# A transformer layer on one Trainium2 core: block sums stored in two parts, and the last layer norm and last product reordered

## The reference, cut to what matters

```python
def layer_norm(x, g, b):
    mu = x.mean(-1, keepdims=True)
    var = jnp.square(x - mu).mean(-1, keepdims=True)
    return (x - mu) * lax.rsqrt(var + EPS) * g + b

y_x = concat([mo, go, co]) @ w_o
x = layer_norm(ALPHA * x + mx[:, 2] * y_x, ln1_g, ln1_b)
u = x * (1.0 + mx[:, 4]) + mx[:, 3]
y_x = jnp.square(jax.nn.relu(u @ w1)) @ w2
x = layer_norm(ALPHA * x + mx[:, 5] * y_x, ln2_g, ln2_b)
```

## Time and profile before

| what | us |
|---|---|
| median of 3 runs | 3297.54 |
| lowest and highest run | 3292.43, 3299.11 |
| the profiled execution | 3291.43 |
| its span in the profile | 3289.6 |
| TensorE busy | 3093.5 (94%) |
| VectorE busy | 2354.3 (72%) |
| GpSimd busy | 1470.7 (45%) |
| ScalarE busy | 1365.4 (42%) |

### The profile page before, as it was taken

How to read it: one execution, slowest core, us unless ns; L and a number is a source line. 1 busy time by engine, 2 the same in 40 slices (tenths; PEclk the granted TensorE clock), 3 DMA queues, 4 the chain that set the end, 5 groups by cost and what they waited for, 6 DMA issues and landing times. The chain is left out here.

```text
span 3289.6 us, 38729 instructions
## 1 busy us (share of the span) xinstructions
PE 3093.5 (94%) x13713; PEld 2283.2 (69%) x13713; DVE 2354.3 (72%) x3209; ACT 1365.4 (42%) x1931; POOL 1470.7 (45%) x857
## 2 busy tenths in 40 slices
PE   6999958999999999999998897999999999999996
PEld 3888845565565655656565775888788888887885
DVE  4344447777777777777765888777778768887778
ACT  3222222434344343444442435655555554344432
POOL 1233301576665766765662445333333223444453
PEclk8999977999999999999998998999999999999998
DMA  6222378123332223230214577444734488777873
GB/s 236 62 88 85 90 239 271 53 57 83 87 82 74 56 61 87 67 80 14 54 35 165 224 260 292 161 158 156 291 144 150 152 311 293 289 265 275 299 288 137
DMA packets 235708, 515.51 MB, mean 157 GB/s; under 512 B 26704, under 2 KB 101840, under 8 KB 223312
## 3 DMA queue, kind: packets, MB, share of 16 engines
q1 hardware_dynamic: 224688, 472.39, 43.0%
q10 hardware_dynamic: 10848, 40.90, 3.5%
HBM read 356.64 MB, written 156.57 MB: 156 GB/s over the span
## 5 line engine op out<-in xcount | busy, mean ns | idle before, releaser
L1032 DVE TENSOR_REDUCE h_mpart<-a_mx 128x1 f32<-128x512 f32 x920 | 568.3, 636 | 260.6 <-PE a_mx L1121 251.7
L978 POOL TENSOR_TENSOR a_acc_p<-a_acc_p,a_pf 128x1024 f32<-128x1024 f32 x240 | 582.0, 2425 | 234.2 <-ACT a_pf L1014 213.0
L1014 ACT ACTIVATE a_pf<-a_sc 128x1024 f32<-128x1024 f32 x432 | 443.0, 1026 | 475.5 <-PE a_sc L1147 470.2
L2148 PE MATMUL f_bank<-slot_hi,f_wx 128*128 128x512 f32 x1280 | 401.0, 390 | 9.0 <-DVE f_wx L1931 7.0
L2081 POOL TENSOR_TENSOR f_work<-raw_rows 128x512 f32<-128x512 f32 x160 | 220.9, 1382 | 369.8 <-DVE f_wx L1931 366.4
L2090 POOL TENSOR_TENSOR f_y<-f_y,raw_rows 128x1024 f32<-128x1024 f32 x80 | 222.0, 2776 | 333.2 <-DMA raw_rows<-in_w 333.2
L2148 PE MATMUL f_bank<-slot_lo,f_wx 128*128 128x512 f32 x896 | 350.0, 391 | 0.0
L2148 PEld LDWEIGHTS f_bank<-slot_hi,f_wx 128*128 128x128 f32 x1280 | 240.9, 188 | 60.4 <-DVE f_wx L1931 7.4
L2156 PE MATMUL f_bank<-slot_hi 128*128 128x512 f32 x672 | 263.9, 393 | 12.4 <-DVE slot_lo L1938 12.4
L1952 DVE TENSOR_TENSOR f_work<-f_work,f_bank 128x512 f32<-128x512 f32 x256 | 174.4, 681 | 134.3 <-ACT f_work L1821 123.1
L2156 PE MATMUL f_bank<-slot_lo,slot_hi 128*128 128x512 f32 x672 | 263.6, 392 | 0.0
(11 more groups left out here) (288 smaller groups left out, 6545.1 us busy)
## 6 DMA issues: line engine op xcount, KB each, us to landing
raw_rows<-s_hx SPq DMA_DIRECT2D x112, 512.0 KB, 4.1
f_y<-in_w SPq DMA_DIRECT2D x112, 512.0 KB, 5.2
raw_rows<-in_w SPq DMA_DIRECT2D x80, 512.0 KB, 5.8
raw_rows<-in_w SPq DMA_DIRECT2D x32, 1024.0 KB, 4.8
s_hx<-stream SPq DMA_DIRECT2D x128, 256.0 KB, 2.7
s_hx<-f_work SPq DMA_DIRECT2D x96, 256.0 KB, 2.0
a_wa<-in_w_ada SPq DMA_DIRECT2D x8, 2048.0 KB, 9.0
s_mix<-low SPq DMA_DIRECT2D x96, 128.0 KB, 2.5
```

The lines of the kernel that those rows point to most:

```text
L978: nc.gpsimd.tensor_tensor(acc[:, :], left[:, :], pf[(b * KT + kt) % NPF][:, :], ALU.add).then_inc(added_p, 1)
L1014: nc.scalar.activation(pf[n % NPF][:, :], sc[n % 2][:, :], ACT.Exp, scale=SCALES[0 if is_mla(b) else 1]).then_inc(exped, 1)
L1032: nc.vector.reduce_max(mpart[b % 2][:, s, k:k + 1], mx[c % 2][:, 0:CHUNKS[k][1]], AX.X).then_inc(mx_read, 1)
L2148: mm = nc.tensor.matmul(by_pair(bank[:, m % 8, :]), w[:, k], x[s][:, :, k * P:(k + 1) * P], start=(k == 0 and j == 0), stop=(k == 3 and j ...
```

## The change

In the mixing stage the seven positions of pair p are made in two parts (`HALVES`): positions 0 to 3 behind tile 2p + 2, positions 4 to 6 behind tile 2p + 3, on GpSimd, ScalarE and VectorE, and their stores likewise. On ScalarE, `stream` of an even tile stands behind the root and the second part of the next tile. `load_m` goes from ScalarE's queue to SyncE's, ahead of the store of `x1`.

In the MLP's second half the products come in another order; the layer norm is two instructions on VectorE (subtract mean, times `ln_g`; times the root, plus `ln_b`), so that ScalarE's centring, GpSimd's addition and two small steps of `norms` are gone; of the last product the first three chunks are made for all four token tiles and the other five tile by tile; its quarter gets gate and residual ahead of it (`before_last`), and then only the gated bank is added; stores of the output count on three semaphores, so that the first copies of the second half wait for their own four tiles.

```diff
+        HALVES = (range(0, 4), range(4, NP))
@@ sync
+            load_m(0)
             sp.dma_start(ln_cols[:, :], a["ln1_cols"]).then_inc(cols_in, 16)
+            load_m(1)
...
             for s, t in enumerate(TILE):
+                if s + 2 < TT:
+                    load_m(s + 2)
                 sp.wait_ge(x1_set, s + 1)
                 sp.dma_start(g.x1[t * P:(t + 1) * P, :], x1[s % 2]).then_inc(x1_stored[s % 2], 16)
...
+                if s >= 2:
+                    store_sums(s // 2 - 1, s % 2)
@@ scalar
             for s in range(TT):
-                if s:
-                    stream(s - 1)
-                act.wait_ge(var_set, s + 1)
-                nc.scalar.activation(rstd[:, :], var[:, :], ACT.Sqrt).then_inc(std_set, 1)
+                if s and s % 2 == 0:
+                    stream(s - 1)
+                root(s)
+                if s >= 2:
+                    highs(s // 2 - 1, s % 2)
+                if s % 2:
+                    stream(s - 1)
                 if s + 2 < TT:
                     load_x(s + 2)
-                    load_m(s + 2)
-                if s and (s - 1) % 2:
-                    highs((s - 1) // 2)
@@ vector
                 work(s)
-                if s and (s - 1) % 2:
-                    lows((s - 1) // 2)
+                if s >= 2:
+                    lows(s // 2 - 1, s % 2)
@@ gpsimd
-                if s and (s - 1) % 2:
-                    sums((s - 1) // 2)
+                if s >= 2:
+                    sums(s // 2 - 1, s % 2)
@@ stage_mlp
-        ORDER2 = (5, 3, 2, 4, 1, 6, 7)
+        ORDER2 = (2, 4, 3, 1, 6, 5, 7)
-        DVE_ADDS = {5: (), 3: (("12", 1),), 2: (("22", -1),), 4: (("11", 1), ("21", 1)), 1: (("11", 1), ("22", 1)), 6: (("22", 1),), 7: (("11", 1),)}
-        ACT_FIRST = {5: (("12", 1), ("11", -1)), 3: (("22", 1),), 2: (("21", 1),), 4: (), 1: (), 6: (), 7: ()}
+        DVE_ADDS = {2: (), 4: (("21", 1),), 3: (("22", 1),), 1: (("11", 1), ("22", 1)), 6: (("22", 1),), 5: (("12", 1), ("11", -1)), 7: (("11", 1),)}
+        ACT_FIRST = {2: (("21", 1), ("22", -1)), 4: (("11", 1),), 3: (("12", 1),), 1: (), 6: (), 5: (), 7: ()}
-        PRES = {3: ("12",), 4: ("21",), 6: ("22",), 7: ("11",)}
+        PRES = {4: ("21",), 6: ("22",), 5: ("12",), 7: ("11",)}
@@ vector, scale
-                dve.wait_ge(centred, k + 1)
-                nc.vector.tensor_tensor(yacc[t], yacc[t], ln_g, ALU.mult).then_inc(scaled, 1)
+                nc.vector.scalar_tensor_tensor(out=yacc[t], in0=yacc[t], scalar=mv[:, t, 0:1], in1=ln_g, op0=ALU.subtract, op1=ALU.mult).then_inc(centred, 1)
+                dve.wait_ge(centred, k + 1)
+                nc.vector.scalar_tensor_tensor(out=yacc[t], in0=yacc[t], scalar=rstd[:, t:t + 1], in1=ln_b, op0=ALU.mult, op1=ALU.add).then_inc(scaled, 1)
@@ vector, last
+                    dve.wait_ge(tt_done, 4 * LAST + tt + 1)
+                    nc.vector.tensor_tensor(part, bank[:, 4 * (LAST % 2) + tt, :], gate[:, 0:512], ALU.mult).then_inc(last_mid, 1)
+                    dve.wait_ge(last_mid, tt + 1)
+                    nc.vector.tensor_tensor(y, y, part, ALU.add).then_inc(add_set, 1)
...
+                    norms(1, tt, 1, k)
+                    scale(1, tt)
@@ tensor
+            for c in range(TOGETHER):
+                cc = LAST * CH + c
+                pe.wait_ge(clo, 2 * cc + 2)
+                for f in range(2):
+                    for tt in range(4):
...
+                        two(LAST, tt, chunk_slot(cc), f, c == 0 and f == 0, False)
             for tt in range(4):
-                for c in range(CH):
+                for c in range(TOGETHER, CH):
```

More of the change, by code:

```diff
@@ L1323, in _, with load_m @@
         def _(sp):
+            def load_m(s):
+                t = TILE[s]
+                if s >= 2:
+                    sp.wait_ge(y_done, s - 1)
+                for part, m in enumerate((m_hi, m_lo)):
+                    sp.dma_start(raw(m[s % 2]), g.mix[part][t]).then_inc(mix_in[s % 2], 16)
+            load_m(0)
             sp.dma_start(ln_cols[:, :], a["ln1_cols"]).then_inc(cols_in, 16)
+            load_m(1)
             for k in range(KD):
@@ L1335, in _, with store_sums @@
                 sp.dma_start(g.raw[:, q], a["w1"][q]).then_inc(mlp_in, 16)
+            def store_sums(p, part):
+                for pos in HALVES[part]:
+                    use = ring_use(p, pos)
+                    if use is None:
+                        continue
+                    sp.wait_ge(lo_set, NP * p + pos + 1)
+                    for level, at in enumerate((ring_hi, ring_lo)):
+                        sp.dma_start(g.uc[p // 4, pos, level][:, p % 4, :], raw(at[use % RING])).then_inc(uc_stored[use % RING], 16)
             for s, t in enumerate(TILE):
+                if s + 2 < TT:
+                    load_m(s + 2)
                 sp.wait_ge(x1_set, s + 1)
                 sp.dma_start(g.x1[t * P:(t + 1) * P, :], x1[s % 2]).then_inc(x1_stored[s % 2], 16)
[L1339 to L1347, removed]
+                if s >= 2:
+                    store_sums(s // 2 - 1, s % 2)
             sp.wait_ge(cols_in, 16)
@@ L1357, in _ @@
         def _(act):
[L1358 to L1363, removed]
             def load_x(s):
@@ L1385, in stream, with highs @@
                 last.then_inc(u_set, 1)
-            def highs(p):
-                for pos, i in enumerate(ORDER):
-                    first, second, sign = right_parts(u, i)
+            def highs(p, part):
+                for pos in HALVES[part]:
+                    first, second, sign = right_parts(u, ORDER[pos])
                     hi, lo = target(p, pos)
@@ L1457, in work, with lows @@
                 assert seen[0] == STEPS, seen
-            def lows(p):
-                for pos, i in enumerate(ORDER):
-                    first, second, sign = right_parts(u, i)
+            def lows(p, part):
+                for pos in HALVES[part]:
+                    first, second, sign = right_parts(u, ORDER[pos])
                     hi, lo = target(p, pos)
@@ L1629, in stage_mlp, with steps @@
         AHEAD, EARLY = 5, 2
-        def steps(prep, evacuate, before_ln, finish, last):
+        TOGETHER = 3
+        def steps(prep, evacuate, before_ln, finish, last, before_last=lambda tt: None):
             ready = EARLY
@@ L1649, in steps @@
                             before_ln(hf, key, tt, pr)
-                elif k < 6 and i in FINISH:
-                    finish(hf, FINISH[i], k - 4)
+                elif k < 6:
+                    if i in FINISH:
+                        finish(hf, FINISH[i], k - 4)
+                    if pr == LAST - 1:
+                        for tt in (2 * k - 8, 2 * k - 7):
+                            before_last(tt)
             last()
@@ L1890, in first @@
                     if hf:
[L1891 removed]
+                        act.wait_ge(out_stored[int(key[0]) - 1], 16 * 4)
                     elif pr == 0:
@@ L1908, in before_ln @@
                     root(hf, FINISH[PRODS[pr][1]][0], 4)
-            def finish(hf, tiles, k):
-                for t in tiles[2 * k:2 * k + 2]:
-                    centre(hf, t)
             def last():
@@ L1916, in last @@
                     root(1, t, 1)
-                    centre(1, t)
-            steps(chunk_high, first, before_ln, finish, last)
+            steps(chunk_high, first, before_ln, lambda *_: None, last)
         @block.vector
@@ L2112, in _ @@
                     tail(n, pos)
-            def bias(hf, t):
-                k = finish_index(hf, t)
-                pool.wait_ge(scaled, k + 1)
-                pool.wait_ge(rows_in, 32)
-                nc.gpsimd.tensor_tensor(yacc[t], yacc[t], ln_b, ALU.add).then_inc(biased, 1)
-            def finish(hf, tiles, k):
-                for t in tiles[2 * k:2 * k + 2]:
-                    bias(hf, t)
-            def last():
-                for t in range(3):
-                    bias(1, t)
-            steps(chunk_sum, lambda *_: None, lambda *_: None, finish, last)
+            steps(chunk_sum, lambda *_: None, lambda *_: None, lambda *_: None, lambda: None)
         @block.tensor
```

79 lines of the change are left out of this document (39 added, 40 removed).

## The result

The median went from 3298.32 us (four runs, 3292.43 to 3303.3) to **3322.88 us** (four runs, 3320.29 to 3325.08): +24.6 us, a ratio of 1.0073 with a 95% interval of 1.0060 to 1.0087. The forecast was 3308.6 us, slower, with a range from 3289 to 3325. The profiled executions lie further apart, 3291.43 and 3323.26 us (spans 3289.6 and 3321.1), because that of before is a low one of its kernel. By stages, cut at the first transpose of the mixing stage, at the first matmul of each half of the MLP and at the end: mixing 244.5 to 281.7 us (+37.2), the MLP's first half 624.5 to 623.8, its second 656.4 to 651.3 (-5.1).

What follows compares the result with a forecast made beforehand. VectorE, not TensorE, paces mixing; late GpSimd sums, then VectorE at the end, bound the MLP's second half. Span 3289.6 + 34.8 - 23.7 = 3300.7, 3302.5 with surroundings, +11.1; carried to the median 3308.6 us, range 3289 to 3325.

Steps and rivals of the forecast that it cites:

- The ring of waits: Mixing stage: stream, turn, stream, sums, VectorE and part 1 wait in a circle; 31.95 or 33.95 us a pair, +34.8 us.
- Forecast B: Mixing stage: GpSimd's additions fall beside VectorE's PSUM-read or single-input steps; 25.8 us a pair, total -38 us; chance 0.20.
- The rule of the port: Mixing stage: two-input VectorE and SBUF-reading GpSimd instructions exclude each other; without it -14 us, blocked once more per part +49.
- the first pair starts from 1816.75, unchanged: Start of the mixing stage: the first pair begins as before; + 6.0 = 1822.75, + 12.95 = 1835.7.
- The load of `mix`: Mixing stage: SyncE issues it about 16 us before use; TensorE's 16.7 us of waits go but gain nothing.
- MLP, term (1): MLP's second half: `ln_b` additions leave GpSimd's queue, so chunk sums no longer come late and TensorE's gaps go; -11.9 us.
- I count the order itself at nothing, hidden by that lead: MLP's second half: the new product order costs nothing, hidden by TensorE's lead of up to five chunks, 27 us.
- MLP, term (2): MLP's end: VectorE's chain from 64.3 to 48.7 us, 15.6 less, against its arrival 3.8 later; -11.8 us.
- A: Whole kernel, the forecast itself: the mixing ring outweighs the MLP's gain; 3302 to 3318 us; chance 0.50.
- rival C: MLP: VectorE's 20 us of added instructions make it the new bound; 6 of 23.7 us come back, +29; chance 0.12.
- no gap near product 8: MLP's second half, a sign of being right: TensorE's gap there is gone.
- Rival D: MLP's end: VectorE is in time, so the MLP gives 37.7 us and the total is -3; chance 0.18.

Runs made afterwards that it cites:

- e5: The changed kernel with GpSimd's addition of `ln_b` in the mixing stage cut to 8 of 1024 columns: 3302.71 us, ratio 1.0009 to before.
- e7: Before's mixing stage with `load_m` on SyncE instead of ScalarE, `ln_cols` ahead of it, and the changed MLP: 3360.69 us, ratio 1.0174 to before.
- e3: The kernel before with only the new product order of the MLP's second half and its tables: 3300.64 us, ratio 1.0005 to before.
- e2: Before's mixing stage with the changed MLP: 3282.94 us, ratio 0.9950 to before.
- e4: Before's mixing stage with the changed MLP, but in the old product order: 3287.87 us, ratio 0.9968 to before.
- e1: The changed mixing stage with the MLP of the kernel before: 3338.61 us, ratio 1.0121 to before.
- e9: e2 with products 4 and 2 exchanged in the MLP's new order: 3286.92 us, ratio 0.9981 to before.
- e12: Before's mixing order, layer norm on VectorE, sums in the low ring; changed MLP, product 4 ahead of 2 in the second token half only: 3274.66 us, ratio 0.9940.

## Why the prediction was right, and where it was off

**The ring of waits: right in mechanism and size.** Forecast were 31.95 and 33.95 us a pair, measured 31.6 and 34.3. Step by step from the end of part 1 (1837.8): the sums start at +8.1 (forecast 8.05), VectorE's tile is over at +13.1 (13.0), part 0 takes 5.7 us (6.0), tile O 7.6 (7.6), part 1 5.2 (5.35). In the last pairs tile O begins 21.6 us after the end of part 1 (21.0 was taken). TensorE's waits before the turns of odd tiles inside the ring are 5.3 to 7.8 us (5 or so forecast), all ended by `stream`. Forecast B, parts that pack, had its additions fall beside other work; e5 shows that they cost 24 us of the stage. The bound for VectorE blocked once more in each part wasn't reached.

**The rule of the port** is borne out by rows: 4.58 us for two low parts beside an addition and a sum, 2.39 without the addition, 1.28 alone. The Trainium skill, page "SBUF — State Buffer", section "Who interferes with whom", says that two such instructions exclude each other and the later one blocks fully; the trace agrees with its 4.58 us.

**Missed: 2.6 us at the start of the stage.** The first sums start at 1814.34, not at 1811.78. The prediction said "the first pair starts from 1816.75, unchanged". SyncE's first two loads of `mix` now stand around the load of `ln_cols` and ahead of the rest of `w_o`, whose first transfer goes out at 1774.41 instead of 1769.61. That this is the cause isn't shown. For it: the `stream` that completes the first pair comes 44.8 us after the stage's start in e7, with `ln_cols` ahead, as before (44.6; 44.4 to 46.3 in the six others that load as before, but for e3 with before's order of loads), and 47.1 to 47.5 in all four kernels with `ln_cols` between the loads. Against it: in e3, with before's mixing stage and its order of loads, it comes at 47.5 too, though `w_o` goes out as early as before (1769.01). The cause stays open. Mixing as a whole: forecast +34.8, measured +37.3 at the next stage's first ScalarE instruction (2044.08 against 2006.81).

**The load of `mix`: right for this kernel, for a narrower reason than given.** "They gain nothing, because TensorE is not in the ring" held. "About 16 us before use, behind at most six stores" holds only in two parts; in one part the same queue costs 71 us (e7 against e2).

**MLP, term (1), -11.9: right in the old order, not in the new.** In e4 no gap is left ahead of the last product, where before there were two, of 2.0 and 6.2 us, in product 8, and the last product starts 565.9 us after the second half's start, against 578.1: 12.2 earlier. (Product 8 took 55.7 us before and an undisturbed one 43.5. The gaps are 8.2 of the difference; the granted clock in that stretch was 0.88.) In the new order the last product starts at 575.3, only 2.8 earlier, and e3 shows the order alone on the old layer norm: gaps grow from 16.4 (20.2 in e1) to 29.2 us. So "I count the order itself at nothing, hidden by that lead" failed for TensorE. "The same product order as regards sums" holds for the number of chunks with sums in a row and not for their place: the old order has two products without sums, 5 and 2, as the first and the third behind the turn of the halves, the new one has only 2 there, as the first, and four products with sums in a row behind it. Whether that place is the reason is open (e9 for it, e12 against it).

**MLP, term (2), -11.8: mis-sized by 9 us, because the work was moved and not removed.** It measured -2.4. Times from the start of the second half, "last additions" being those for the product before the last:

| kernel | last product starts | VectorE begins the last additions | from there to its end | second half |
|---|---|---|---|---|
| before | 578.1 | 589.0 | 64.3 | 656.4 |
| forecast | 566.2 | 580.9 | 48.7 | 632.7 |
| changed | 575.3 | 596.6 | 51.6 | 651.3 |
| e2, new order | 572.4 | 596.0 | 51.5 | 650.6 |
| e4, old order | 565.9 | 583.8 | 63.3 | 650.3 |

The chain at VectorE's end held nearly as worked out, 12.7 us shorter (forecast 15.6). VectorE's arrival there did not: forecast was 8.1 us earlier than before (-11.9 + 3.8), measured 7.6 later. The step that failed is "Against that VectorE comes to this point later, by the 5 us above less the port waits saved: 3.8". The finish of four tiles, which the forecast took out of the chain, is not gone; the new order does it ahead of the additions. VectorE in e4, where it stands behind them, and in e2:

```profile
3223.20 1.27 DVE L2011 TENSOR_TENSOR f_work<-f_work,f_bank 128x512 f32<-128x512 f32 x2
...
3241.51 1.28 DVE L2042 SCALAR_TENSOR_TENSOR f_work<-f_work,cond_pad,f_ln_g 128x1024 f32<-128x1024 f32 x1
```

```profile
3206.75 1.28 DVE L2042 SCALAR_TENSOR_TENSOR f_work<-f_work,cond_pad,f_ln_g 128x1024 f32<-128x1024 f32 x1
...
3235.75 2.47 DVE L2011 TENSOR_TENSOR f_work<-f_work,f_bank 128x512 f32<-128x512 f32 x4
```

From e4 to e2 the chain is 11.8 us shorter and the arrival 12.2 later. The finish itself is eight instructions of 1.28 us, 10 us; a wait of 3.7 us for a load (3258.91) also stands in e4's chain, and one of 5.3 us ahead of e2's. The two gains that the forecast added, an early last product and a short chain, were each seen, in different orders, and never together.

This second wait is 5.3 us in the changed kernel too (1.48 + 3.81; e2 1.54 + 3.72): two stores of the output (SyncE, 3249.66, 4.88 us of issuing) wait for scaled rows, the next chunk's loads stand behind them (3255.34), GpSimd waits 8.62 us for these, and the high and the low part follow (3264.14, 3265.23). That these stores are the cause is read from the order of the queue. It was argued, not shown: a kernel with the stores behind one more chunk's loads wasn't tried.

**The sum.** Forecast were +34.8 - 23.7, measured in the profiles +37.2 - 5.1, and by the ratios of e1 and e2 +40 - 16. The direction was earned, by the ring. The size was not: +24.6 us by medians is more than twice the +11.1 forecast, 3322.88 lies outside A's own 3302 to 3318, and the stated range holds it only because it was drawn out to rival C. Of the signs named, "no gap near product 8" failed (3.6 us at 3040.26), and one of the signs of being wrong came true in part: gaps stand in products 8 and 10 (1.3 us) now. Rival C priced the loss in the MLP about right for the profile (6 of 23.7 us come back) and too high by the medians (8 of 23.7 are missing there); its reason, VectorE as the new bound, is true of the end and not of the middle, where e4 has no gaps with the same added instructions. Rival D fell: VectorE came later, not in time.

## What to carry to other kernels

Splitting a batch of work in two so that it starts earlier puts every wait of the batch into the ring twice; draw the ring with each queue in it before you split, and price it: here it was right to 0.4 us. Work that is moved ahead of the last chain is not gone: before you book a shorter chain, ask when its engine now arrives there, and don't add to it what another engine gains. Moving a load from one queue to another is to be judged by what stands ahead of it there, not by the load.

## What the runs showed of the hardware that was not expected

VectorE's small steps on one column wait for GpSimd as large ones do. The two-input steps at L1454 and L1455 take 0.16 us each alone (1861.44, 1861.63) and 1.05 and 1.22 beside GpSimd's two sums (1845.94, 2.54 us), so a correction of a root in five tiny steps pays 2 us when sums are released with the root. And here the two engines take turns: the two low parts of 4.58 us (1851.51) hold the rest of an addition (to 1853.84), one low part, the sum that was next on GpSimd (1.74 us at 1853.80, where one alone is 1.27), and only then the second low part, so that two instructions of 0.6 us met two waits.
